# Weight slots of the first expert round in other places, and regrouped work at the start, in both attentions and at the end

## The reference

```python
h = rmsnorm(x, ln_mix); z = h @ w_in            # q, f (two directions), v, og, c_q, c_kv, k_rope, gates
o_hg = gla(q, 1-f, v, log f) + gla(reversed)    # gated linear recurrence, 4 heads of 128, output gate silu(og)
y_a = (rmsnorm(o_hg) * silu(og)) @ w_oA
q = rope(rmsnorm(rmsnorm(c_q) @ w_uq)); k, v = from rmsnorm(c_kv) @ w_ukv, k_rope
y_b = softmax(q k^T / sqrt(96)) v @ w_oB        # MLA: 8 heads, values of 64
x = x + (sigmoid(gate_a) * y_a + sigmoid(gate_b) * y_b) @ w_out
hm = rmsnorm(x)
x = x + moe(hm)      # top group of 8, then top 2 of its 8 experts; silu(x w1) * (x w3) @ w2, width 256
x = x + (p @ w_ple_proj) * sigmoid(rmsnorm(x) @ w_ple_gate)
```

```python
sh, sc, gt = silu(c) @ w_mod + b_mod            # also for the 256 context rows, with c_ctx
h = rmsnorm(x) * (1 + sc) + sh; parts = h @ w_in     # 10 parts of 1024 columns
y_a = (silu(z_a) * b * dwconv3(c * x_in)) @ w_out_conv
# 16 heads of 64, grid of 4 rows x 64 columns: a query sees the keys of all 4 rows in
# 16 columns around its own (with a bias), and all 256 context keys
y_b = (silu(z_b) * softmax([q k_window^T + bias, q k_ctx^T]) [v_window; v_ctx]) @ w_out_attn
y = (sigmoid(g_a) * y_a + sigmoid(g_b) * y_b) @ w_o
x = x + gt * rmsnorm(y)
```

## Time and profile before

| | us |
|---|---|
| three runs | 1205.39, 1206.57, 1209.9 (median 1206.57) |
| profiled execution | 1204.21 |
| its span | 1202.4 |
| TensorE busy | 1150.9 (96%) |
| DVE busy | 509.0 (42%) |
| ACT busy | 237.1 (20%) |
| POOL busy | 107.3 (9%) |
| DMA | 324.57 MB, mean 270 GB/s |
| chain that ended last | TensorE 76%, DMA 9%, DVE 3%, ACT 1%, POOL 1% |

### The profile page before, as it was taken

How to read it: one execution, slowest core, us unless ns; L and a number is a source line. 1 busy time by engine, 2 the same in 40 slices (tenths; PEclk the granted TensorE clock), 3 DMA queues, 4 the chain that set the end, 5 groups by cost and what they waited for, 6 DMA issues and landing times.

```text
span 1202.4 us, 13070 instructions
## 1 busy us (share of the span) xinstructions
PE 1150.9 (96%) x5176; PEld 663.1 (55%) x5176; DVE 509.0 (42%) x848; ACT 237.1 (20%) x446; POOL 107.3 (9%) x116
## 2 busy tenths in 40 slices
PE   6999999999999999999989898899999999999997
PEld 6877888858434454544433233354447854456643
DVE  2146348465120202011111120376765676577677
ACT  2122654203000001000000000121001011048801
POOL 0016136000000000000000000000000020035300
PEclk9999999999999999999999999899999999999999
DMA  9999323377899999999999999954446445453300
GB/s 318 344 300 347 109 71 106 106 295 321 359 422 414 406 408 421 413 413 422 413 421 421 421 422 422 356 176 166 147 141 209 140 160 207 140 171 127 104 3 35
DMA packets 116950, 324.57 MB, mean 270 GB/s; under 512 B 8736, under 2 KB 62112, under 8 KB 92320
## 3 DMA queue, kind: packets, MB, share of 16 engines
q1 hardware_dynamic: 111152, 316.32, 69.1%
q0 software_dynamic: 1536, 4.20, 1.1%
q10 hardware_dynamic: 4208, 3.31, 0.9%
HBM read 322.76 MB, written 1.05 MB: 269 GB/s over the span
## 4 chain that ended last, share of the span: by engine, by line
PE 76%; DMA 9%; DVE 3%; issue 1%; ACT 1%; POOL 1%; SPq 0%; DVEq 0%; POOLq 0%
PE bank L731 23%; PE bank L1050 16%; PE bank L710 14%; DMA AR<-in_w 8%; PE bank L1091 6%; PE bank L1026 2%; PE bank L1065 2%; PE bank L1062 2%; DMA ring<-in_w 1%; PE bank L1198 1%; PE bank L713 1%; PE bank L1231 1%; PE bank L1211 1%; PE bank L1129 1%; PE bank L1077 1%
## 5 line engine op out<-in xcount | busy, mean ns | idle before, releaser
L710 PE MATMUL bank<-HT,ring 128*128 128x256 f32 x864 | 192.6, 380 | 0.0
L1050 PE MATMUL bank<-ring,AR 128*64 128x512 f32 x608 | 172.6, 610 | 15.5 <-DMA AR<-in_w 9.7
L710 PEld LDWEIGHTS bank<-HT,ring 128*128 128x128 f32 x864 | 162.1, 190 | 28.3 <-issue 7.4
L2171 DVE TENSOR_TENSOR AR<-AR,bank 128x256 f32<-128x256 f32 x32 | 13.5, 421 | 273.3 <-ACT AR L1460 272.8
L1050 PE MATMUL bank<-AR 128*64 128x512 f32 x416 | 125.8, 605 | 2.0 <-DMA AR<-in_w 1.8
L731 PE MATMUL bank<-ring,AR 128*128 128x512 f32 x280 | 124.2, 602 | 2.4 <-DVE AR L1755 1.2
L1050 PEld LDWEIGHTS bank<-ring,AR 128*64 128x64 f32 x608 | 50.6, 139 | 106.3 <-issue 103.2
L731 PE MATMUL bank<-ring,HN 128*128 128x512 f32 x224 | 97.3, 592 | 0.0
L731 PEld LDWEIGHTS bank<-ring,AR 128*128 128x128 f32 x280 | 53.3, 193 | 69.5 <-issue 67.2
L1091 PE MATMUL bank<-ring,AR 128*64 128x512 f32 x352 | 79.6, 594 | 0.0
L731 PE MATMUL bank<-ring,HT 128*128 128x512 f32 x168 | 73.7, 592 | 0.0
(11 more groups left out here) (357 smaller groups left out, 1378.7 us busy)
## 6 DMA issues: line engine op xcount, KB each, us to landing
ring<-in_w SPq DMA_DIRECT2D x120, 1024.0 KB, 16.7
AR<-in_w SPq DMA_DIRECT2D x72, 1024.0 KB, 15.0
ring<-in_w_in SPq DMA_DIRECT2D x61, 1024.0 KB, 7.0
ring<-in_w_mod SPq DMA_DIRECT2D x12, 1024.0 KB, 9.8
AR<-in_w_in SPq DMA_DIRECT2D x6, 1024.0 KB, 18.1
ring<-in_w_out SPq DMA_DIRECT2D x4, 1024.0 KB, 5.0
ring<-in_w_ple_gate SPq DMA_DIRECT2D x4, 1024.0 KB, 9.9
AR<-in_bias POOLq DMA_DIRECT2D x32, 128.0 KB, 2.4
```

The source lines that it names most:

```text
L710: mm = pe.matmul(bank[:, part * T:part * T + T], w[:, k, c0 + part * P:c0 + part * P + P], act[:, k, :], start=(k == 0), stop=(k == k_n - 1))
L1050: mm = pe.matmul(bank[e * SLOT:e * SLOT + SLOT, :].rearrange("p (w n) -> p w n", w=2), XG[:, k, :], w, start=(k == 0), stop=(k == DK - 1))
L2171: V_.tensor_tensor(SGM[:, p % 2], SGM[:, p % 2], bank[:, 0:FE], ALU.mult).then_inc(S("moe_silu"), 1)
```

## The change

**Start.** Fill 0 comes in two halves, in turn with the halves of xT; of the constants only `ident` and `ones` come then, the others behind fill 1, and the tables of cos, sin and window mask as late as the C fills. `cq` is computed in two halves of k, each for both parts of the rows, and `ckv`'s first part stands ahead of the diagonal product.

**Modulation.** The gate rows have two half banks of their own.

**MLA.** DVE normalises the weights before they are transposed. The values are computed for pairs of heads, already transposed, and DVE copies them into `OTM`; the transposes of `OM` and ACT's copies are gone. ACT makes the copies of the recurrence's first two levels.

**Expert slots.** A new area `LATE` of 1 MB holds router weights and small tables first and is a nineteenth slot in round 0, for j = 20, issued at `rank_ps`. j = 21 takes the place of j = 14 and waits for its use; the other extra slots have other numbers in round 1.

**Scatter.** TensorE counts up `scat_ps` behind each half of the scatter, and DVE waits for each.

**Second block.** From its input on, the second block's tokens are in groups of eight grid columns. A query tile of 128 then meets 416 of the 512 keys (`met`), and scores, maximum, exponent and scaling have 416 columns. The context's keys are copied by ACT to the middle of the key rows. The eighth gate stands behind the attention's loop. x is fetched anew in that order by 32 small DMAs, and the result is stored in pieces of 128 KB, six on SP and two on ACT, when both halves of a token tile are done.

```diff
-                for f in range(NA):
+                for f in range(1, NA):
 ...
+            for half in range(2):
+                sp.dma_start(XT[:, ks, :], a["xT"][:, ks, :]).then_inc(S(f"x_in{half}"), 16)
+                sp.dma_start(slot_view(0)[:, ks, :], fills[0][0][:, ks, :])...
+            sp.dma_start(X, ...); sp.dma_start(CST[:, 0:FIRST], a["consts"][:, 0:FIRST])
 ...
-            product(of["cq"][0], XT, ahead=...)
+            for ks in (range(4), range(4, 8)):
+                for part in range(2):
+                    product(of["cq"][0], XT, parts=(part,), ks=ks, ...)
+            product(of["ckv"][0], XT, parts=(0,))
 ...
-            product(of["ckv"][0], XT)
+            product(of["ckv"][0], XT, parts=(1,))
 ...
                 if u >= 8:
-                    wait_bank(i)
+                    pe.wait_ge(S("emptied_act"), emptied[of["mod"][max(u - 2, 7)]][1])
 ...
             def mla_values(c):
+                for kt in range(TT):
+                    for e in range(2):
+                        h = 2 * c + e
+                        mm = pe.matmul(B[c % 2][e * VD:e * VD + VD, 0:T], KV[:, kt, h * P + NOPE:h * P + P],
+                                       PT[:, e, kt, :], start=(kt == 0), stop=(kt == TT - 1))
 ...
-        EXTRA = {0: 12, 1: 6}
+        EXTRA = {(0, 12): 0, (0, 13): 1, (0, 14): 2, (0, 15): 3, (0, 16): 4, (0, 17): 5, (0, 20): 6, (0, 21): 2,
+                 (1, 6): 0, (1, 7): 1, (1, 10): 4, (1, 11): 5}
 ...
-                return EXTRA[0] + x + 1 if r else None
+                past = [q * NM + i + 1 for (q, i), y in EXTRA.items() if y == x and (q, i) < (r, j)]
+                return max(past, default=None)
 ...
-            for j in (4, 5, 0, 1, 2, 3, 12, 13, 14, 15, 16, 17, 6, 7, 8, 9, 10, 11):
+            for j in (4, 5, 0, 1, 2, 3, 12, 13, 14, 15, 16, 17, 6, 7, 8, 9, 10, 20, 11):
 ...
+                elif j == 20:
+                    sp.wait_ge(S("rank_ps"), 1)
 ...
-            for j in range(18, NM):
+            for j in (18, 19, 21, 22, 23):
                 sp.wait_ge(S("moe_used"), used_before(j, 0))
                 expert_dma(j, 0, 0)
 ...
-                    sp.wait_ge(S("moe_used"), NM + EXTRA[1] + (3, 0)[n] + 1)
+                    sp.wait_ge(S("moe_used"), (16, NM + 7)[n])
 ...
-                mm.then_inc(S("scat_ps"), 1)
+                    mm.then_inc(S("scat_ps"), 1)
 ...
+        def met(t):
+            return slice(t * (T - NEAR), t * (T - NEAR) + T + NEAR)       # NEAR = 160
 ...
-                V_.tensor_tensor_reduce(PR2[:, n % 4, :], B[2 + n % 4][:, :], BM[:, n % 4, :], -1.0, 3e38,
+                V_.tensor_tensor_reduce(PR2[:, n % 4, m], B[2 + n % 4][:, m], BM[:, n % 4, m], -1.0, 3e38,
 ...
-                if n % 4 == 1:
+                if n % 4 == 1 and n < 28:
                     attention_gate(n // 4)
                 turned_weights(n)
+            attention_gate(7)
 ...
             for t in range(TT):
-                for half in range(2):
-                    sp.wait_ge(S("final"), 2 * t + half + 1)
-                    sp.dma_start(out[0, t * P:t * P + P, c], HN[:, t, c]).then_inc(S("stored"), 16)
+                sp.wait_ge(S("final"), 2 * t + 2)
+                for g in range(4 if t == 0 else 2):
+                    store(sp, t, g)
```

More of the change, by code:

```diff
@@ L89, in constants @@
     put("sinT", np.sin(ang.astype(np.float64)) * np.where(i % 32 < 16, -1.0, 1.0)[:, None])
[L90 to L94, removed]
+    col = BY_COLUMNS % GW
+    for tile in range(2):
+        qc, kc = col[tile * P:tile * P + P], col
+        start = np.clip(qc - WIN // 2, 0, GW - WIN)
+        inside = (kc[None, :] >= start[:, None]) & (kc[None, :] < start[:, None] + WIN)
+        at = CONST_COLS["winmask"][0] + tile * T
+        c[:, at:at + T] = np.where(inside, 0.0, -1e30)
     put("invfreq", 10000.0 ** (-np.arange(16, dtype=np.float32) / np.float32(16)))
@@ L467, in bank_of, with part_bank @@
             return B[bank_no[i]]
+        def part_bank(i, part):
+            return B[4] if i == of["cq"][0] and part else bank_of(i)
         def bank_before(i):
@@ L587, in nth, with grid_rows, store @@
             return seq.index(tag) + 1
+        def grid_rows(v):
+            return v.rearrange("p (g r c) -> p r g c", r=T // GW, c=8)
+        def store(queue, t, g):
+            rows = out[0].rearrange("(r g c) d -> g r c d", r=T // GW, c=8)
+            queue.dma_start(rows[4 * t + g], HN[32 * g:32 * g + 32, t, :]).then_inc(S("stored"), 16)
         block = ctx.enter_context(nc.Block())
@@ L893, in mla_turn, with mla_values @@
                 mm.then_inc(S("mla_pT"), 1)
[L895 to L902, removed]
+            def mla_values(c):
+                pe.wait_ge(S("mla_pt"), 2 * c + 2)
+                if c >= 2:
+                    pe.wait_ge(S("mla_o"), c - 1)
+                for kt in range(TT):
[3 more added lines that the diff above has]
+                                       PT[:, e, kt, :], start=(kt == 0), stop=(kt == TT - 1))
                 mm.then_inc(S("mla_pv"), 1)
@@ L967, in _ @@
             pe.wait_ge(S("gla_o"), 1)
-            products("yb", OTM, ahead=pairs_of("omT"))
+            products("yb", OTM)
             pe.wait_ge(S("normed"), nth("o", NORMED))
@@ L1400, in _, with gla_copy @@
                     gate_copy(1 + h // 2, ACT.Sigmoid)
+            def gla_copy(n):
+                act.wait_ge(S("gla_s"), n + 1)
+                for st in range(TT):
+                    ins = nc.scalar.activation((AXX, AD)[n][:, st], B[GLA_BANKS[n] + st][:, :].rearrange("p (h t) -> p h t", h=GH),
+                                               ACT.Copy)
+                ins.then_inc(S("gla_a"), 1)
             gla_exp(1)
+            gla_copy(0)
             for n in range(2, len(LEVELS) - 1):
                 gla_exp(n)
+                if n == 2:
+                    gla_copy(1)
                 if n in (3, 4, 6):
@@ L1411, in _ @@
                                  ACT.Sigmoid).then_inc(S("sig"), 1)
-            act.wait_ge(S("omT_ps"), 1)
-            for c in range(2):
-                nc.scalar.activation(OTM[:, 2 * c:2 * c + 2, :].rearrange("p a t -> p (a t)"), B[4 + c][:, :], ACT.Copy)\
-                  .then_inc(S("omT"), 1)
             act.wait_ge(S("gla_o"), 1)
@@ L1562, in exp2 @@
                 act.wait_ge(S("na_nmax"), n + 1)
[L1563 removed]
+                pr = PR2[:, n % 4, met(n // 2 % 2)]
+                nc.scalar.activation(pr, pr, ACT.Exp, scale=-1.0, bias=NMX2[:, n % 4:n % 4 + 1],
                                      accum_out=SUM2[:, n % 4:n % 4 + 1]).then_inc(S("na_p"), 1)
@@ L1597, in _ @@
                       .then_inc(S("y_sq"), 1)
+            act.wait_ge(S("final"), 2 * TT)
+            for g in range(2, 4):
+                store(act, TT - 1, g)
+            act.wait_ge(S("stored"), 16 * TT * 4)
         M_TMP_K = area(M0, 4, TT, MH * 16)
@@ L2426 @@
     table = np.where(held[None], rpb[:, dr, np.clip(dc, 0, 2 * WIN - 2)], np.zeros((), rpb.dtype))
-    arrays["bias"] = table
+    arrays["bias"] = table[:, BY_COLUMNS][:, :, BY_COLUMNS]
     arrays["consts"], arrays["masks"] = constants()
```

221 lines of the change are left out of this document (138 added, 83 removed).

## The result

The changed kernel takes 1213.78 us (median of 5, 1212.86 to 1214.56), the kernel before 1205.39 beside it (median of 5, 1204.31 to 1209.9): a ratio of 1.0072, 95% interval 1.0056 to 1.0088. It is slower by 0.7%; the forecast was 1207.0 and no change. The profiled execution took 1213.51 with a span of 1211.7, 9.3 more than before.

What follows compares the result with a forecast made beforehand. The full load stream was taken to bound the MoE's end, TensorE nearly all else. Terms -2.8 - 2.0 - 3.2 + 12.7 - 1.0 - 4.0 + 0.7 = +0.4 gave 1204.6 profiled, 1207.0 us in the runs' frame (1202.5 to 1211.5).

Steps and rivals of the forecast that it cites:

- the end: Output stores: 512 KB leave together on two queues after the last result, +0.7 us (0 to +1.5).
- MoE: Expert loads: SP's wait at load 21 blocks those behind it, the stream is empty for 15.0 us, +12.7 (10.5 to 13.5).
- The credit of 2.5 for the new slot: Expert loads: load 20 leaves earlier and fills a hole, so the later stream has one load less, -2.5 us.
- Start: First products: half fills let TensorE begin at 6.75 instead of 9.57, -2.8 us (-1.5 to -3.5).
- modulation: Modulation banks: own banks for the gate rows remove TensorE's wait for DVE, -2.0 us (0 to -2.0).
- first attention: MLA: fewer value groups and no transposes of the outcome, DVE's extra multiplication hidden, -3.2 us (-4 to 0).
- the wait of 2.08 that I took as kept: First attention: TensorE's wait for DVE's operands at 195.78, through POOL, ACT and DVE, stays at 2.08 us.
- Scatter: Behind the MoE: DVE's additions start after the first four products instead of all eight, -1.0 us (0 to -1.0).
- second attention: Second block: 416 of 512 columns save 3.2 us, the gate's later place 0.8; together -4.0 (-5 to 0).
- The faster one: MoE: the empty stretch doesn't reach the end; 1192 us, or 1199.4 with half recovered; chance 0.17.
- the slower one: MoE: TensorE waits for loads, runs cold and frees slots late, so the stream runs dry again; 1214 to 1216 us; chance 0.18.
- The third one: Both attentions: saved products turn into waits, 0 for both; 1213 us; chance about 0.05, counted with slower.

Runs made afterwards that it cites:

- plain rows: Changed kernel with each output store of 32 rows writing rows that follow each other in memory, so output rows are in wrong places: 1208.0 us, ratio 1.0015.
- the wait alone: Kernel before with only load 21 of round 0 changed, to wait for the 15th use instead of the 4th: 1216.01 us, ratio 1.0091.
- the longer wait: Changed kernel with load 21 of round 0 waiting for the 18th use instead of the 15th: 1225.37 us, ratio 1.0162.

## Why the prediction was wrong

- **The failed step is the end.** "Now 512 KB leave together ... some 1.2 us of data at the loads' 421 GB/s" was priced at +0.7 with an upper end of 1.5; it is +6.6. I took the rate of loads with 128 outermost rows for stores with 4. No row of before shows a store of that shape, so the upper end should have come from the slowest transfer at hand, not from the fastest. The runs put 5.4 of the 6.6 on the shape, whose 4 groups leave 4 of 16 DMA engines at work (9.06 to 3.64 behind the last result with plain rows), and 1.2 on the later departure and the issues, for which +0.7 (0 to 1.5) was a fair term. With +6.6 the same sum gives 1212.9 and "slower"; and with plain rows the changed kernel measured 1208.0, a ratio of 1.0015, which is the forecast's "no change".
- **MoE, right.** +12.3 for +12.7: the stretch without loads was 14.8 for 15.0, it came from SP's order, TensorE had no wait in round 0, and the lead of early rounds paid for nothing. The credit of 2.5 for the new slot is in that sum and bought nothing: the run with the wait alone has no new slot and the same MoE, for there the empty stretch is 12.9 instead of 14.8. A load that leaves earlier only lets the stream run dry earlier.
- **Start, modulation, first attention: -4.9 for -8.0.** The modulation's wait went (-2.0, right). The start gave -1.6 in the profiled pair: the first half of the weights landed at 7.3, not 6.6, and the first 11 matmuls ran at half speed instead of 8. Over the traces of all runs the f product begins at 23.1, 23.9 and 23.7 with the old start and at 20.5 to 22.0 with the new (mean of 8: 21.3), so the term is -2.3 and the profiled execution alone is one draw. The first attention gave -1.3 for -3.2. Of the 2.9 for the values 1.5 came: 0.9 is the multiplication that I called hidden, 0.3 the four value groups at 1.01 instead of 0.94 (1.88 for 16 matmuls is not twice the time of 8 between other work), and 0.3 to 0.4 the transposes before each of them, 0.53 or more to the next operation instead of 0.44. The transposes behind the recurrence gave 0.9, but the next product then waits for DVE and 0.6 of it is lost (0.35 forecast). And the wait of 2.08 that I took as kept became two, 1.01 and 1.45: another 0.4.
- **Scatter and second attention** were -0.8 and -3.4 for -1.0 and -4.0. The wait of 0.7 before the last values stayed.
- **The frame.** I added 2.4 for the median of three runs. With two more the median is 1205.39, so the shift is 1.2, and for the changed kernel it is 0.3. In the profiled pair the forecast was +0.4 and +9.3 came: 5.9 of the difference is the end, 3.1 the start to the first expert product.
- **Rivals.** The faster one is refuted by the two runs with the wait alone or longer. Of the slower one only the lower clock is seen (0.96 from 330 to 450, and 0.93 from 350 to 450 with the longer wait); the stream stayed full beside it, at 1.02, so it cost nothing. The third one's price was added up wrong: the two attentions are 3.2 and 4.0, so 7.2 and not 6.

Terms on one side that cancel others of the same size (-13.0, +13.4) made a forecast of no change look safe. Its error was the sum of theirs, and all but two of them (the MoE and the second block's part ahead of the attention, 0.4 each) erred to the same side.

## What to carry to other kernels

A wait in a queue that issues loads in order costs what stands behind it, not what it guards: place a load that must wait behind every load that needn't. Where a stream of loads is the bound, look for the stretch in which it is empty before you count what TensorE saves; a new slot for an earlier load pays only if the stream doesn't run dry, or wait for TensorE to hand places back, further on. A store's rate is that of its shape: before it is reordered, count its outermost dimension.

## What was not expected of the hardware

- Stores of 128 KB as 4 groups of 8 rows moved 86 GB/s over their last 9.1 us at a DMA share of 0.23, with 4 packets moving at a time; as 32 rows that follow each other they had 16 packets moving and ended 3.6 us behind the result.
- With TensorE's granted clock at 0.93 from 350 to 450, the stream of loads kept its share of 1.02: the longer wait cost its own 13.0 us in the MoE and nothing on top.
- The first matmuls of each execution ran at half speed (0.43 us each instead of 0.22, which is the lower level, 1.2 GHz, though the windows' granted clock reads 1.00 there). This lasted for 7 to 14 matmuls, 3.1 to 6.2 us, over the eleven traces, which alone moves the start by over 1 us.
